# Three feed-forwards in parts of 8, 6 and 8 tiles, with seven block products in 9 of 22 gate-and-up jobs

## The reference

```python
D_MODEL, SEQ, D_FF = 1024, 512, 2816

# first block
h = rms_norm(x, norm_ffn_g[l]) * (1.0 + sc2) + sh2
gt, up = jnp.split(jnp.einsum("bsd,df->bsf", h, w_ffn_up[l]), 2, axis=-1)
x = x + g2 * jnp.einsum("bsf,fd->bsd", jax.nn.silu(gt) * up, w_ffn_down[l])

# both layers of the second block
def conv_glu_ffn(h, w_up, conv_w, conv_b, w_down):
    S = h.shape[1]
    a, b = jnp.split(h @ w_up, 2, axis=-1)
    a_pad = jnp.pad(a, ((0, 0), (CONV_WIDTH_2 - 1, 0), (0, 0)))
    a = sum(conv_w[j] * a_pad[:, j:j + S] for j in range(CONV_WIDTH_2)) + conv_b
    return (jax.nn.silu(a) * b) @ w_down
```

## Time and profile before

| what | us |
|---|---|
| median of 3 executions | 2096.95 |
| lowest and highest | 2092.3, 2097.04 |
| the profiled execution's own time | 2093.53 |
| its span, first to last instruction | 2091.7 |
| PE busy in the span | 2059.9 |
| DVE, ACT, POOL busy | 989.1, 885.9, 840.6 |
| mean granted clock of TensorE | 0.998 of 2.4 GHz |

### The profile page before, as it was taken

The page is one execution under the profiler, slowest core; times in us unless marked ns, Lnnn a source line. Parts: engine busy times, 40 slices in busy tenths (PEclk is TensorE's granted clock), DMA queues, the critical chain, the costliest instruction groups (busy, mean ns, idle before and its releaser), DMA issues.

```text
span 2091.7 us, 28578 instructions
## 1 busy us (share of the span) xinstructions
PE 2059.9 (98%) x10618; PEld 1735.8 (83%) x10618; DVE 989.1 (47%) x1909; ACT 885.9 (42%) x1307; POOL 840.6 (40%) x273
## 2 busy tenths in 40 slices
PE   9999999999999999999999999999999999999998
PEld 6888977888888888876877888888887588888887
DVE  4889788574311111376985344034323934431432
ACT  3355545463443222534366453233423954432332
POOL 3443422444244444433713443444443044444443
PEclk9999999999999999999999999999999999999999
DMA  9654322325232432432202433333422034324322
GB/s 371 243 185 125 102 62 66 101 85 178 81 100 81 114 107 78 113 93 65 79 24 64 113 100 93 107 105 94 143 86 73 2 96 121 100 80 121 100 70 91
DMA packets 304008, 220.17 MB, mean 105 GB/s; under 512 B 13520, under 2 KB 288080, under 8 KB 301616
## 3 DMA queue, kind: packets, MB, share of 16 engines
q1 hardware_dynamic: 293216, 195.67, 31.1%
q10 hardware_dynamic: 10704, 23.33, 3.7%
HBM read 213.48 MB, written 2.10 MB: 103 GB/s over the span
## 4 chain that ended last, share of the span: by engine, by line
PE 85%; DVE 7%; issue 3%; ACT 2%; POOL 2%; DMA 0%; ACTq 0%; DVEq 0%; SPq 0%; POOLq 0%
PE bank L912 72%; PE bank L1159 2%; PE bank L1375 2%; PE bank L1353 2%; DVE arena L2811 1%; PE bank L1307 1%; DVE small L2809 1%; PE bank L1362 1%; PE bank L1458 1%; PE bank L1207 1%; POOL w_split_out L2851 1%; DVE bank L2277 1%; POOL w_split L2851 1%; PE bank L1218 1%; PE bank L1540 1%
## 5 line engine op out<-in xcount | busy, mean ns | idle before, releaser
L912 PE MATMUL bank<-h_hi,w_split 128*128 128x512 f32 x3696 | 1119.4, 382 | 1.8 <-DVE arena L2679 1.1
L2851 POOL TENSOR_TENSOR w_split<-wslots,w_split 128x2048 fp32r<-128x2048 f32 (+3 forms) x174 | 712.7, 4097 | 987.9 <-ACT w_split L1613 549.5
L912 PEld LDWEIGHTS bank<-h_hi,w_split 128*128 128x128 f32 x3696 | 698.7, 189 | 116.8 <-issue 15.7
L912 PE MATMUL bank<-h_lo,w_split 128*128 128x512 f32 x1848 | 701.8, 380 | 0.0
L912 PEld LDWEIGHTS bank<-h_lo,w_split 128*128 128x128 f32 x1848 | 349.7, 189 | 51.2 <-issue 3.4
L912 PE MATMUL bank<-hid_hi,w_split 128*128 128x512 f32 x1056 | 316.2, 380 | 2.2 <-DVEq L2562 2.2
L1634 ACT ACTIVATE w_split<-wslots 128x2048 fp32r<-128x2048 f32 (+2 forms) x80 | 141.4, 1767 | 368.0 <-PE bank L912 368.0
L1613 ACT ACTIVATE w_split<-wslots 128x2048 fp32r<-128x2048 f32 (+3 forms) x91 | 158.8, 1745 | 300.8 <-PE bank L912 278.9
L912 PEld LDWEIGHTS bank<-hid_hi,w_split 128*128 128x128 f32 x1056 | 199.6, 189 | 32.3 <-issue 3.6
L912 PE MATMUL bank<-hid_lo,w_split 128*128 128x512 f32 x528 | 200.1, 379 | 0.0
L2277 DVE SCALAR_TENSOR_TENSOR bank<-arena,cols,bank 128x512 f32<-128x512 f32 x240 | 161.3, 750 | 5.4 <-ACT bank L1727 4.9
(11 more groups left out here) (341 smaller groups left out, 2352.4 us busy)
## 6 DMA issues: line engine op xcount, KB each, us to landing
wslots<-in_f_w_up SPq DMA_DIRECT2D x88, 512.0 KB, 4.7
wslots<-in_w_in SPq DMA_DIRECT2D x24, 1024.0 KB, 5.3
wslots<-in_w_ffn_up SPq DMA_DIRECT2D x44, 512.0 KB, 4.5
arena<-in_w_ada ACTq DMA_DIRECT2D x8, 2048.0 KB, 9.1
wslots<-in_f_w_down SPq DMA_DIRECT2D x16, 768.0 KB, 4.8
wslots<-in_a_w_in SPq DMA_DIRECT2D x10, 1024.0 KB, 5.2
wslots<-in_f_w_down SPq DMA_DIRECT2D x16, 640.0 KB, 4.4
arena<-in_w_ada_first SPq DMA_DIRECT2D x8, 1024.0 KB, 19.3
```

Of the source, the lines that this page charges most:

```text
L912: return nc.tensor.matmul(bank[:], w, woven(x), start=start, stop=stop)
L2851: last = nc.gpsimd.tensor_tensor(part[:, 1, cols_of], slot(p, 1, size)[:, 0, cols_of], part[:, 0, cols_of].bitcast(F32), ALU.subtract)
```

## The change

**Parts.** Each feed-forward is cut in parts of 8, 6 and 8 tiles. A down stage of the first two parts has 4 jobs of two output tiles (2 x 8 x 3 or 2 x 6 x 3 products); the last has 8 jobs of one tile, 8 chunks each, and begins with `last_downs`: job 1 writes the second bank of job 0's slot and waits for `lo_ready` alone, and job 2 is split in two halves by ACT and POOL.

**Seven products.** In 9 of the 11 even jobs of each feed-forward (the *units*: the even job of pairs 2 and 3 of part 0, of pairs 0 to 2 of part 1, of pairs 0 to 3 of part 2) the product is computed as a two-by-two block product: the weights as four blocks of (gate or up) x (first or second four chunks), the activations as four blocks of (first or second four tiles) x (256 of the 512 tokens). Instead of eight block products there are seven (the Winograd form of Strassen's scheme), each 4 chunks times 3 products, 256 columns wide: 84 products. For them DVE makes four sums of weight blocks (`three_sums`, `fourth_sum`, 128x512 each, both inputs in SBUF), ACT rounds seven operands and POOL subtracts seven times (128x512 each), in place of one rounding and one subtraction of 128x2048. Afterwards ACT copies one block product, DVE adds it up in `early_sums` (while the last three products run) and `late_sums` (four additions of 256 columns behind the last).

**Token sums.** Once for each feed-forward, four sums of activation blocks, 128x1024 each, are made by DVE, rounded by ACT and subtracted by POOL. For k of 1 and 2, ACT first copies the 8 tiles with their gain (`whole_tokens`), and both that and DVE's four sums stand in their streams ahead of the square root and the reciprocal.

**Loops.** ACT, DVE, PE and POOL write the feed-forwards out instead of looping. SP's queue keeps its order: the same gate-and-up loads, and down loads of the same bytes in fewer and larger jobs.

The diff, cut to these:

```diff
-HALVES = ((0, 12), (12, FT - 12))
+PARTS = ((0, 8), (8, 6), (14, FT - 14))
+LAST = len(PARTS) - 1
+DOWN = [P if part == LAST else 2 * P for part in range(len(PARTS))]
+SEVEN = (0, 1, 2)
...
+def seven_at(k, part, i):
+    return k in SEVEN and (0 if part else 2) <= i < PARTS[part][1] // 2
...
+                start_split(name, 0)
+                tiles(p, 0, kc - 1)
+                if k == 0:
+                    tiles(p, kc - 1, kc)
+                pe.wait_ge(lo_ready[other], SPLITS_BEFORE[FIRST[name] + 1] + 1)
+                tiles(other, 0, kc - 3)
+                if k:
+                    tiles(p, kc - 1, kc)
+                tiles(other, kc - 3, kc)
+                _, use = one(name, 2)
+                pe.wait_ge(bank_free[p], use + 1)
...
+            def seven_products(k, part, i):
+                name, unit = f"ffn{k}_up{part}", (k, part, i)
+                q, use = one(name, 2 * i)
+                pe.wait_ge(bank_free[q], use + 1)
+                for e, bank, at, tokens in ((0, 7, 0, 2), (1, 7, 1, 0), (2, 6, 1, 1), (4, 6, 0, (0, 0)), (3, 2 * q, 1, (1, 1)), (5, 2 * q, 0, (1, 0)), (6, 2 * q + 1, 0, 3)):
+                    if e < 6:
+                        pe.wait_ge(S["sums_lower"], LOWER[unit] + e + 1)
+                    else:
+                        pe.wait_ge(lo_ready[q], SPLITS_BEFORE[FIRST[name] + 2 * i] + 1)
+                    for c in range(DT // 2):
+                        for wp, hp in ((0, 0), (0, 1), (1, 0)):
+                            if isinstance(tokens, int):
+                                x = token_sums[tokens][hp][:, 2 * c:2 * c + 2, :].rearrange("p a b -> p b a")
+                            else:
+                                x = woven(h_split[hp][:, DT // 2 * tokens[0] + c, :])[:, tokens[1] * P:(tokens[1] + 1) * P, :]
+                            last = nc.tensor.matmul(banks[bank][:, at * HALF:(at + 1) * HALF], entries[k][e][wp][:, c, :], x,
+                                                    start=c == 0 and wp + hp == 0, stop=c == DT // 2 - 1 and wp == 1)
+                    if e in (3, 4):
+                        last.then_inc(S["g_turned_then_products"], 1)
+                last.then_inc(product_done[q], 1)
+            def up_part(k, part):
+                name = f"ffn{k}_up{part}"
+                for i in range(JOBS[name] // 2):
+                    if i == part == 0:
+                        waits = ("late_ready", LATE_TILES[f"ffn{k}"]) if k else ("norm_ready", TILES_BEFORE["ffn0"])
+                        split_job(start_split(name, 0), DT, 2 * P, h_parts, waits, late=f"ffn{k}" if k else None)
+                    elif seven_at(k, part, i):
+                        seven_products(k, part, i)
+                    else:
+                        split_job(start_split(name, 2 * i), DT, 2 * P, h_parts, None)
+                    split_job(start_split(name, 2 * i + 1), DT, 2 * P, h_parts, None)
...
+            def sum_uppers(k, part, i):
+                for e, made in enumerate((1, 3, 4, 4)):
+                    act.wait_ge(S["angle_then_sum_ready"], SUMS[k, part, i] + made)
+                    nc.scalar.activation(entries[k][e][0][:], entry_sums[k][e], ACT.Copy).then_inc(S["softplus_then_sums_upper"], 1)
+            def block_uppers(k, part, i):
+                n = FIRST[f"ffn{k}_up{part}"] + 2 * i
+                act.wait_ge(weights_in[n % 2], LOADED[n])
+                act.wait_ge(product_done[n % 2], slot_before(n) // 2 + 1)
+                for e, block in ((4, (0, 0)), (5, (0, 1)), (6, (1, 1))):
+                    nc.scalar.activation(entries[k][e][0][:], block_of(k, *block), ACT.Copy).then_inc(S["softplus_then_sums_upper"] if e < 6 else hi_ready[n % 2], 1)
...
+            def first_product(k, part, i):
+                act.wait_ge(S["g_turned_then_products"], PRODUCTS[k, part, i] + 1)
+                nc.scalar.activation(up_gate[:, 1 - FF_PARITY[k], 0:HALF], banks[6][:, 0:HALF], ACT.Copy).then_inc(S["softplus_then_sums_upper"], 1)
+            def token_upper(k, j):
+                act.wait_ge(S["angle_then_sum_ready"], SUMS[k] + (3 if j in (2, 0) else 4))
+                nc.scalar.activation(token_sums[j][0][:], token_plain[j], ACT.Copy).then_inc(S["softplus_then_sums_upper"], 1)
+            def whole_tokens(k):
+                for c in range(DT):
+                    act.wait_ge(S["late_x"], LATE_TILES[f"ffn{k}"] + c + 1)
+                    last = nc.scalar.activation(tokens_of(c), token_rows(xT[:, c, :]), ACT.Copy, scale=late_gain(f"ffn{k}", c))
...
+                        if following:
+                            sum_uppers(*following)
+                            block_uppers(*following)
+                        else:
+                            split_job(slot_after(FIRST[name] + 2 * i))
+                        first_pair = i == part == 0 and k in SEVEN
+                        if first_pair and k:
...
+                made(1)
+                sum_of(2, 1, 2)
+                made(2)
+                sum_of(1, 1, 0)
+                made(3)
+                sum_of(3, 3, 1)
...
+            def three_sums(k, part, i):
+                n = FIRST[f"ffn{k}_up{part}"] + 2 * i
+                dve.wait_ge(weights_in[n % 2], LOADED[n])
+                before = UNITS.index((k, part, i)) - 1
+                if before >= 0:
+                    dve.wait_ge(S["g_turned_then_products"], PRODUCTS[UNITS[before]] + 1)
+                sum_of_blocks(k, 0, block_of(k, 0, 0), block_of(k, 1, 0), ALU.subtract)
+                sum_of_blocks(k, 1, block_of(k, 1, 0), block_of(k, 1, 1), ALU.add)
+                dve.wait_ge(S["angle_then_sum_ready"], SUMS[k, part, i] + 2)
+                sum_of_blocks(k, 2, entry_sums[k][1], block_of(k, 0, 0), ALU.subtract)
+            def fourth_sum(k, part, i):
+                dve.wait_ge(S["angle_then_sum_ready"], SUMS[k, part, i] + 3)
+                sum_of_blocks(k, 3, block_of(k, 0, 1), entry_sums[k][2], ALU.subtract)
...
+                first, sums = up_gate[:, 1 - FF_PARITY[k], :], up_gate[:, FF_PARITY[k], :]
+                dve.wait_ge(S["softplus_then_sums_upper"], UPPER[k, part, i, "first"])
+                steps.did(nc.vector.tensor_tensor(first[:, HIGH], banks[6][:, HIGH], first[:, LOW], ALU.add))
+                steps.settle()
+                both = first[:, HIGH].rearrange("p (a b) -> p a b", a=1).to_broadcast([P, 2, HALF])
+                steps.did(nc.vector.tensor_tensor(halves(sums), both, halves(banks[7][:]), ALU.add))
+            def late_sums(k, part, i):
+                q, use = one(f"ffn{k}_up{part}", 2 * i)
+                first, sums = up_gate[:, 1 - q, :], up_gate[:, q, :]
+                gates, ups = banks[2 * q], banks[2 * q + 1]
+                dve.wait_ge(product_done[q], use + 1)
+                steps.settle()
+                steps.did(nc.vector.tensor_tensor(gates[:, LOW], gates[:, LOW], first[:, LOW], ALU.add))
+                steps.did(nc.vector.tensor_tensor(gates[:, HIGH], gates[:, HIGH], sums[:, HIGH], ALU.add))
+                steps.did(nc.vector.tensor_tensor(ups[:, LOW], ups[:, LOW], sums[:, LOW], ALU.add))
+                last = nc.vector.tensor_tensor(ups[:, HIGH], banks[7][:, HIGH], sums[:, LOW], ALU.add)
...
+            def up_part(k, part, turn):
+                name, tiles = f"ffn{k}_up{part}", PARTS[part][1]
+                for i in range(tiles // 2):
+                    following = (k, part, i + 1) if seven_at(k, part, i + 1) else None
+                    unit = seven_at(k, part, i)
+                    if unit and i == 0:
+                        early_sums(k, part, 0)
+                    if following:
+                        three_sums(*following)
+                        if unit:
+                            dve.wait_ge(S["g_turned_then_products"], PRODUCTS[k, part, i] + 2)
+                        else:
+                            q, use = one(name, 2 * i)
+                            dve.wait_ge(product_done[q], use + 1)
+                        fourth_sum(*following)
+                    if unit:
+                        late_sums(k, part, i)
+                    turn(2 * i, None)
+                    turn(2 * i + 1, (lambda: early_sums(*following)) if following else None)
...
+            def entry_lowers(k, part, i):
+                n = FIRST[f"ffn{k}_up{part}"] + 2 * i
+                for e, block in enumerate((None, None, None, None, (0, 0), (0, 1), (1, 1))):
+                    hi, lo = entries[k][e]
+                    if e < 6:
+                        pool.wait_ge(S["softplus_then_sums_upper"], UPPER[k, part, i, e])
+                    else:
+                        pool.wait_ge(hi_ready[n % 2], SPLITS_BEFORE[n] + 1)
+                    nc.gpsimd.tensor_tensor(lo[:], block_of(k, *block) if block else entry_sums[k][e], hi[:].bitcast(F32),
+                                            ALU.subtract).then_inc(S["sums_lower"] if e < 6 else lo_ready[n % 2], 1)
...
+                for part, (_, tiles) in enumerate(PARTS):
```

(17 more changed lines are left out.)

423 lines of the change are left out of this document (326 added, 97 removed).

## The result

The changed kernel takes 2082.63 us (median of 5 executions, 2078.24 to 2082.9) against 2096.95 (5 executions); the ratio is 0.9931, with 0.992 to 0.9943 as its interval. The prediction was 2090.0 and faster, so the sign is right and the gain is twice the one worked out (14.3 us instead of 6.9). The time lies inside the range of 2077 to 2099, but 3.4 under the 2086 down to which my forecast reached by itself. The profiled execution took 2078.68, its span is 14.8 us shorter than that of before.

What follows compares the result with a forecast made beforehand. TensorE, busy 2059.9 of 2091.7 us, was taken to bound the kernel. The terms -25.1 + 5.6 + 3.5 + 6.4 + 1.3 + 1.3 + 0.1 gave -6.9 us, so 2090 on the median of 2096.95, range 2077 to 2099.

Steps and rivals of the forecast that it cites:

- 27 units: All feed-forwards: 84 products of 256 columns take 9.43 us, saving 0.93 us a unit, 25.1 us in 27.
- steady pairs: Feed-forward 1 and 2: the fourth sum waits out one GpSimd subtraction; TensorE waits 0.7 us in 8 pairs, 5.6 us.
- first job: Feed-forward 1 and 2: token sums delay the reciprocal and scaling; TensorE loses 1.8 us before job 2, 3.5 in both.
- first unit: Feed-forward 1 and 2: DVE's sums alternate with GpSimd's token subtractions; the first unit loses 3.2 us, 6.4 in both.
- part 1 to down: Behind part 1: 6.5 us of products before the last tile, whose chain takes 7.1; 0.6 us each, 1.3 us.
- a_keys: At a_keys: the job ahead takes 5.2 us instead of 6.5, so a wait of 1.7 instead of 0.4, 1.3 us.
- last_downs: Last down stages: removes a 1.10 us wait in both, loses 2.3 in feed-forward 1; +1.2 there, -1.1 in feed-forward 2.
- Half the width costs half: Rival, chance 0.07: a unit's product of 256 columns takes 0.1079 us, saving 35 us, so 2080.
- waits between block products: Rival, chance 0.13: waits inside units cost 0.045 us each, giving 9 us back, so 2098.
- Raw weights most of a pair before the sums want them: Weight loads for units: slot free once GpSimd has subtracted, most of a pair before the sums; listed as costing nothing.
- the port seldom decides: Rival, chance 0.25: sums and subtractions miss one another, the 5.6 and 6.4 us go; -18.9 us, so 2078.
- One more subtraction in DVE's way: Rival, chance 0.10: in 12 pairs of feed-forward 1 and 2 sums wait out a second 1.27 us subtraction; 15 us, 2105.

Runs made afterwards that it cites:

- parts_alone: The changed kernel without its units, every job again 48 products, parts and new last down stage kept: 2099.12 us, ratio 1.0019 to the kernel before.
- fourth_behind: The changed kernel with DVE's fourth weight sum behind the four late sums where unit follows unit in feed-forward 1 and 2: 2089.75 us, ratio 0.9977.
- tokens_split: The changed kernel, feed-forward 1 and 2: first unit at pair 3, token sums behind the first tile, their roundings and subtractions in two pieces each: 2072.91 us, ratio 0.9903.
- first_later: The changed kernel with the first unit of feed-forward 1 and 2 at pair 3 instead of 2, 25 units instead of 27: 2076.37 us, ratio 0.9913.

## Why the prediction was right or wrong

By its terms, predicted and read from the profile after:

| term | predicted | measured |
|---|---|---|
| 27 units | -25.1 | -26.5 |
| steady pairs | +5.6 | 0 |
| first job | +3.5 | +1.9 |
| first unit | +6.4 | +4.2 |
| part 1 to down | +1.3 | +0.4 |
| `a_keys` | +1.3 | +1.3 |
| `last_downs` | +0.1 | 0.0 |
| next stage's first product | none | +0.7 |
| falls of the clock, two for one | none | +1.6 |
| first 17 us of the program | none | +0.8 |
| sum | -6.9 | -15.6 |

The span itself moved by -14.8. Of the 0.8 left, 0.24 are the first 64 products behind the new wait at the next stage (14.05 in the chain, 13.81 before); the rest, mostly 0.2 in each of feed-forward 1 and 2, stays open. The first 17 us are not the change's: the first long run of products starts between 39.8 and 41.1 us in the profiles of this study, at 40.60 here and 39.85 before.

- **The unit**: right, and 0.1117 a product instead of 0.1122. The estimate from the Trainium skill, "TensorE: Matmul & The Clock Gate", Part 2, "Back-to-back issue gap" (109.2 ns, by a formula that the page gives for the isolated product), is further off than the row was (112.2). *Half the width costs half* and *waits between block products* are both refuted by 9.38 in every unit but the first of feed-forward 1 and 2.
- **The steady pair** is the step that failed. Its mechanism is there, a sum that waits out a subtraction (1.58), and so is its order; the sizes around it were each too long. The odd tile's `hid_lo` ended at 7.6 instead of 7.9, the fourth sum at 11.5 instead of 12.0, the roundings at 14.3 instead of 14.7; and the chain from the convolution step to `hid_lo`'s end was taken as 5.5 from the earlier trace rows, whose loop is unrolled by the change: 5.15 now (1436.66 to 1441.81), and as much in `parts_alone`, which is unrolled and has no units. A wait of 0.7 us was made of terms that together could be off by 1, and multiplied by 8. What was lacking was the room beside it: 0.3 us, known only since `fourth_behind`.
- **First job**: the token sums end 12.7 behind the start, exactly as worked out; the chain behind them was again too long (the product starts at 22.8, `bank_free` was put at 23.4), and TensorE came to it at 21.85 instead of 21.6, so 0.95 is left of 1.8. That the sums cause it, `parts_alone` and `tokens_split` show.
- **First unit**: right in kind (5.21 for two sums), 2.1 instead of 3.2.
- **The parts**: `a_keys` right in size, `last_downs` in its sum (+0.8 in feed-forward 1 and -0.8 in 2, where +1.2 and -1.1 were forecast). I said that nothing else in them costs; the stage behind feed-forward 1 does, because two jobs of 24 products (10.4 us) instead of 30 (12.9) now cover a transfer that takes 7.8, with ACT's rounding in front of the tile's copies.
- **"Raw weights most of a pair before the sums want them"** was wrong for the second unit of part 2, where DVE waits 0.17 for them.
- **Rivals**: the time fell between my forecast and *the port seldom decides*, 2078. That rival would have been right for the wrong reason: turns happen in steady pairs and cost TensorE nothing, and at the first unit they do cost. *One more subtraction in DVE's way* did not occur in the steady pairs.
- **The total**: each cost of the units was put too high, so the sign was not luck. That the gain is twice the forecast rests for a good part on 0.3 us of room in the steady pairs, which the prediction did not know of.

## What to carry to other kernels

A wait that is the small difference of two long sums should be given as a room with its error, and tested by pushing the chain by a known amount (1.24 us pushed, 0.95 seen, so 0.3 of room); take the durations for it from code that is unrolled as the new code will be. Work moved off a critical chain is to be cut in pieces and put behind whatever is due next in *each* queue: the same token work made TensorE wait 0.95 twice ahead of the reciprocal, 7.4 twice behind it, 3.7 twice in one piece behind the first tile, and not at all in two pieces. And where shorter jobs replace longer ones, look at every transfer that their length had covered, and at what stands behind it in the waiting engine's queue.

## What the runs showed of the hardware

- A VectorE instruction with two SBUF inputs that meets one of GpSimd lasts about as long as what is left of that one plus its own time: 4.39 + 1.08 for the 5.47 beside 5.06 (1.22 alone), 0.89 + 0.69 for the 1.58. It is not slowed by a share. It goes both ways: a subtraction of GpSimd that met the end of the same sum took 3.33 instead of 2.35.
- The granted clock of TensorE fell to half behind idle times of 0.9 to 2.8 us, mostly for 3.4 us, and cost 1.6 to 1.7 at the three places read; behind the two of 7.4 it was ten and some seven us at half. But the idle of 1.93 ahead of the last down stage was followed by a fall in both profiles of the changed kernel and in neither of `first_later` and `tokens_split`, and the idle of 1.58 that ends at 905.28 in the kernel before by one there, but by none in the changed kernel, where it is as long. What else decides was not found. The profiles have from none to four falls inside the program, so two kernels can differ by several us through them alone.
- The 1 MB load at the end of feed-forward 1 landed 7.8 to 9.5 us behind its issue, where most groups of 1 MB weight loads on the page have a median of 5.1 to 5.5. Another load, 2 MB of the memory's weights, was issued 4.6 us ahead of it; that it is the cause was not tried.
